# Expert stage of a hybrid transformer layer: sixteen expert steps become twelve, ranked on the chip, with six weight buffers

## What is computed

```python
scores = sigmoid(t @ router_w); biased = scores + router_b
grp = biased.reshape(n_tok, 4, 4)
g_sel = argmax(sum(top_k(grp, 2)))               # best group
idx = g_sel * 4 + top_k(grp[g_sel], 2)           # two experts of it
w = scores[idx] / sum(scores[idx])
y = sum_e gates[:, e] * ((silu(t @ w1[e]) * (t @ w3[e])) @ w2[e])
x = x + m5 * y
```

## Time and profile before

| | us |
|---|---|
| median of 3 runs | 928.34 |
| profiled execution, time | 927.07 |
| its span | 925.2 |
| PE busy | 865.7 |
| DVE busy | 383.7 |
| ACT busy | 197.6 |
| POOL busy | 122.8 |

### The profile page before, as it was taken

How to read it: one execution, slowest core, us unless ns; L and a number is a source line. 1 busy time by engine, 2 the same in 40 slices (tenths; PEclk the granted TensorE clock), 3 DMA queues, 4 the chain that set the end, 5 groups by cost and what they waited for, 6 DMA issues and landing times. The chain is left out here.

```text
span 925.2 us, 9791 instructions
## 1 busy us (share of the span) xinstructions
PE 865.7 (94%) x3803; PEld 459.7 (50%) x3803; DVE 383.7 (41%) x805; ACT 197.6 (21%) x435; POOL 122.8 (13%) x109
## 2 busy tenths in 40 slices
PE   4999999999999999999999999999993899999993
PEld 3445476655844445555555554444553444444441
DVE  3239455643345426556675750102236322222221
ACT  3221266100011032322332320100120222111110
POOL 1000000000148300110111111110001022221211
PEclk9899999999999999999999999999985899999997
DMA  8952020300072134262533435205142489999952
GB/s 313 330 193 91 0 91 1 115 1 1 1 250 76 39 99 153 91 205 60 184 98 134 147 136 198 91 0 182 45 168 83 155 269 300 299 305 289 308 148 41
DMA packets 79234, 131.65 MB, mean 142 GB/s; under 512 B 7297, under 2 KB 40786, under 8 KB 79186
## 3 DMA queue, kind: packets, MB, share of 16 engines
q1 hardware_dynamic: 74578, 122.61, 38.9%
q0 software_dynamic: 4608, 8.40, 4.0%
HBM read 126.79 MB, written 12.58 MB: 151 GB/s over the span
## 5 line engine op out<-in xcount | busy, mean ns | idle before, releaser
L468 PE MATMUL ps<-arena 128*128 128x512 f32 (+9 forms) x2962 | 770.6, 451 | 15.1 <-DVE arena L1593 5.7
L468 PEld LDWEIGHTS ps<-arena 128*128 128x128 f32 (+5 forms) x2962 | 360.3, 167 | 375.9 <-issue 355.2
L1022 ACT ACTIVATE arena<-ps 128x512 f32<-128x512 f32 (+5 forms) x132 | 54.7, 439 | 180.3 <-PE ps L468 133.3
L471 PE MATMUL ps<-tab,arena 128*128 128x128 f32 x476 | 67.4, 285 | 14.5 <-DVE arena L1266 6.6
L471 PEld LDWEIGHTS ps<-tab,arena 128*128 128x128 f32 x476 | 58.0, 148 | 42.7 <-issue 34.3
L1436 DVE SCALAR_TENSOR_TENSOR arena<-arena,ps 128x512 f32<-128x512 f32 x32 | 22.0, 687 | 116.7 <-ACT arena L1111 116.5
L1761 POOL TENSOR_TENSOR arena<-arena 128x512 f32<-128x512 f32 x24 | 30.4, 1268 | 279.8 <-DVE arena L1436 279.8
L1726 POOL TENSOR_TENSOR stat<-stat,mhalf 128x1 f32<-128x1 f32 (+2 forms) x20 | 23.2, 1162 | 319.0 <-DVE stat L1241 318.9
L1111 ACT ACTIVATE arena<-ps 128x512 f32<-128x512 f32 x32 | 19.1, 597 | 198.9 <-PE ps L468 198.9
L1684 DVE TENSOR_TENSOR arena<-arena,ps 128x256 f32<-128x256 f32 x16 | 6.7, 422 | 105.5 <-ACT arena L1213 105.5
L1404 DVE SCALAR_TENSOR_TENSOR arena<-arena,cond 128x512 f32<-128x512 f32 x56 | 42.6, 761 | 2.3 <-PE ps L471 0.6
(11 more groups left out here) (149 smaller groups left out, 379.0 us busy)
## 6 DMA issues: line engine op xcount, KB each, us to landing
arena<-in_moe_w SPq DMA_DIRECT2D x32, 1024.0 KB, 10.3
arena<-in_w_in SPq DMA_DIRECT2D x12, 2048.0 KB, 8.9
arena<-in_mod_w SPq DMA_DIRECT2D x16, 1024.0 KB, 5.2
arena<-in_moe_w SPq DMA_DIRECT2D x32, 512.0 KB, 10.7
arena<-in_mod_w SPq DMA_DIRECT2D x4, 2048.0 KB, 16.8
arena<-in_w_out SPq DMA_DIRECT2D x2, 2048.0 KB, 7.9
arena<-in_x SPq DMA_DIRECT2D x4, 512.0 KB, 5.7
arena<-in_w_in SPq DMA_DIRECT2D x2, 1024.0 KB, 18.3
```

The lines of the kernel that those rows point to most:

```text
L468: return nc.tensor.matmul(o, l, r, start=start, stop=stop, skip_group_check=True)
L471: return nc.tensor.transpose(o, i, ident[0:n, 0:n])
L1022: return A_(o, i, ACT.Copy)
```

## The change

The fourteen experts 2 to 15 are ranked on the chip by their number of tokens. Columns 0 and 1 are experts 0 and 1, columns 2 to 7 the six larger of the fourteen, columns 8 to 15 the eight smaller, in the order of their numbers. There are twelve steps: columns 0 to 7 have one each; columns 8 and 12, 9 and 13, 10 and 14, 11 and 15 share one. In a shared step slots 0 to 63 belong to the first expert and slots 64 to 127 to the second; the gather, the transposes, the modulation, silu, the scaling and the add handle both at once, and each matmul with expert weights becomes two, one for each half of the stationary columns, with its own weights and its own half of the PSUM partitions. If one of the eight smaller has more than 64 tokens, one more round follows, in which all sixteen run as before.

There are six weight buffers. Only experts 0 and 1 are loaded before the ranking is known. The other loads wait for `sort_ready`; SP reads each expert's number from `eid` into a register. Loads of columns 2 to 5 have no buffer to wait for, that of column n from 6 on waits for the outputs of the step that used buffer n - 6.

The token lists are made in groups of 2, 4, 4 and 2 steps. The group of experts 0 and 1 comes first; the ranking (`order_by_count`, `place_columns`) and the reordering of slots and gates by column (`permute`) follow on DVE between it and the first hidden layer; the picks of a later group are made one step ahead.

The first round is written out, where a loop stood before. The diff, cut to its core:

```diff
+HALF_CAP = P // 2
 NOBODY = 4096
+KNOWN = 2
+SINGLE = 8
+STEPS = SINGLE + (NE - SINGLE) // 2
+FREE = NE - KNOWN
+SLOTS = 6
+TOKEN_GROUPS = [(0, 2), (2, 4), (6, 4), (10, 2)]
...
+def step_parts(s):
+    if s < SINGLE:
+        return [(slice(0, P), s)]
+    return [(slice(0, HALF_CAP), s), (slice(HALF_CAP, P), s + (NE - SINGLE) // 2)]
+LOAD_COLUMNS = [c for s in range(STEPS) for _, c in step_parts(s)]
+def load_step(n):
+    return n if n < SINGLE else SINGLE + (n - SINGLE) // 2
+def token_group(s):
+    return max(f for f, (first, _) in enumerate(TOKEN_GROUPS) if first <= s)
...
-        at1 = [R_G] + [SLOT * ((N_OUT - 1 + i) % RING) for i in range(3)]
+        at1 = [R_G] + [SLOT * ((N_OUT - 1 + i) % RING) for i in range(3)] + [R_G + 3 * WE, R_QK]
         w13 = [region(a, 2, KD, FE) for a in at1]
         w2 = [[region(a, D), region(b, D)] for a, b in
-              ((R_G + 2 * WE, R_G + 2 * WE + D), (R1 + 2048, R1 + 3072), (2 * WE, SLOT + 2 * WE), (2 * SLOT + 2 * WE, R_V))]
+              ((R_G + 2 * WE, R_G + 2 * WE + D), (R1 + 2048, R1 + 3072), (2 * WE, SLOT + 2 * WE), (2 * SLOT + 2 * WE, R_V),
+               (R_G + 5 * WE, R1 + D), (R1, R1 + 4 * D))]
         rt = region(R_HC, 2048)
         masks = region(R_HC + 1280, P).bitcast(mybir.dt.bfloat16).rearrange("p (a n) -> p a n", a=2)
+        posP, gateP = rt[:, 320:384], rt[:, 980:1036]
+        eid = rt[:, 384:384 + FREE].bitcast(mybir.dt.int32)
...
-                if t == XT - 1:
-                    for n in range(N_OUT, N_LOADS):
-                        sp.wait_ge(ring_used[n % RING], used_value(n))
-                    load_expert(2, 2)
                 sp.wait_ge(xn2_done, t + 1)
                 sp.dma_start(xds[t], xn2[:, t]).then_inc(xs_done, 16)
                 sp.dma_start(os[t], xr[:, t]).then_inc(out_done, 16)
-            sp.wait_ge(hg_in[1], 16)
-            load_expert(3, 3)
-            def weights(r, first=0):
-                with sp.Fori(first, NE // 4) as i:
-                    for q in range(4):
-                        sp.wait_ge(y_mm, NE * r + 4 * i + (q - 3))
-                        load_expert(q, 4 * i + q)
-            weights(0, first=1)
-            sp.wait_ge(out_done, 16 * XT)
+            def expert_of(c):
+                return c if c < KNOWN else sp.value_load(eid[0:1, c - KNOWN:c - KNOWN + 1], min_val=KNOWN, max_val=NE - 1)
+            sp.wait_ge(sort_ready, 1)
+            for n in range(KNOWN, NE):
+                if n == KNOWN:
+                    for m in range(N_OUT, N_LOADS):
+                        sp.wait_ge(ring_used[m % RING], used_value(m))
+                if n == SLOTS - 1:
+                    sp.wait_ge(out_done, 16 * XT)
+                e = expert_of(LOAD_COLUMNS[n])
+                if n >= SLOTS:
+                    sp.wait_ge(y_mm, load_step(n - SLOTS) + 1)
+                load_expert(n % SLOTS, e)
...
+            def picks(f, e, parts):
+                for t in range(XT):
+                    for rows_of, c in parts:
+                        last = mm(ps[rows_of, (7 if f else 3), 5 * e:5 * e + 5], pick[:, e % PICKS, t, rows_of], tokg[:, t, c, :],
+                                  t == 0, t == XT - 1)
+                last.then_inc(pick_mm, 1)
...
+            def hidden(parts, slots):
+                for k in range(KD):
+                    for (rows_of, c), q in zip(parts, slots):
+                        last = mm(ps[rows_of, 2, :].rearrange("p (w f) -> p w f", w=2), hgT[:, k, rows_of], w13[q][:, :, k, :],
+                                  k == 0, k == KD - 1)
+                last.then_inc(h_mm, 1)
+            def outputs(par, parts, slots):
+                for half in range(2):
+                    for f in range(2):
+                        for (rows_of, c), q in zip(parts, slots):
+                            last = mm(ps[rows_of, 4 + 2 * par + half, :], aT[:, f, rows_of], w2[q][f][:, half * 512:(half + 1) * 512],
+                                      f == 0, f == 1)
+                last.then_inc(y_mm, 1)
...
+                pick_group(0)
+                turn_step(0)
+                for s in range(STEPS):
+                    for _, c in step_parts(s):
+                        n = LOAD_COLUMNS.index(c)
+                        pe.wait_ge(moe_in[n % SLOTS], 64 * (n // SLOTS + 1))
+                    pe.wait_ge(hgT_act, s + 1)
+                    pe.wait_ge(hgT_dve, s + 1)
+                    hidden(step_parts(s), slots_of(s))
+                    if s + 1 < len(TOKEN_GROUPS):
+                        pick_group(s + 1)
+                    if s + 1 < STEPS:
+                        turn_step(s + 1)
+                    if s >= 1:
+                        outputs_step(s - 1)
+                    pe.wait_ge(a_done, s + 1)
+                    turn_hidden()
+                outputs_step(STEPS - 1)
...
+            def split_gates(x, first, count):
+                hi, mid = tokg[:, :, first:first + count, 2], tokg[:, :, first:first + count, 3]
+                rest = rt[:, 400:400 + XT * count].rearrange("p (t e) -> p t e", t=XT)
+                link(V.tensor_copy(hi, x))
+                link(V.tensor_tensor(rest, x, hi, ALU.subtract))
+                link(V.tensor_copy(mid, rest))
+                V.tensor_tensor(tokg[:, :, first:first + count, 4], rest, mid, ALU.subtract).then_inc(tokb_ready, 1)
+            split_gates(gate[:, :, 0:KNOWN], 0, KNOWN)
...
+            def order_by_count():
+                link(V.scalar_tensor_tensor(key, total[:, KNOWN:NE], 64.0, erow, ALU.mult, ALU.add))
+                link(V.tensor_tensor(compare, key.unsqueeze(1).broadcast_to(wide), key.unsqueeze(2).broadcast_to(wide), ALU.is_gt))
+                link(V.tensor_reduce(order_of, compare, AX.X, ALU.add))
+            def place_columns():
+                bound = SINGLE - KNOWN - 0.5
+                link(V.scalar_tensor_tensor(key2, order_of, bound, erow, ALU.is_gt, ALU.add))
+                link(V.tensor_tensor(compare, key2.unsqueeze(1).broadcast_to(wide), key2.unsqueeze(2).broadcast_to(wide), ALU.is_le))
+                link(V.tensor_reduce(column, compare, AX.X, ALU.add))
+                link(V.tensor_tensor(chosen, const("iota")[:, 0:FREE].unsqueeze(2).broadcast_to(wide),
+                                     column.unsqueeze(1).broadcast_to(wide), ALU.is_equal))
+                link(V.tensor_tensor(compare, chosen, eidx.unsqueeze(1).broadcast_to(wide), ALU.mult))
+                link(V.tensor_reduce(eidf, compare, AX.X, ALU.add))
+                V.tensor_copy(eid, eidf).then_inc(sort_ready, 1)
+            def permute(o, x):
+                work = rt[:, 1040:1040 + XT * FREE * FREE].rearrange("p (t c e) -> p t c e", t=XT, c=FREE)
+                for t in range(XT):
+                    last = V.tensor_tensor(work[:, t], chosen, x[:, t:t + 1, KNOWN:NE].broadcast_to(wide), ALU.mult)
+                link(last)
+                link(V.tensor_reduce(o, work, AX.X, ALU.add))
...
+                link(V.tensor_scalar(small64[:, KNOWN:NE], order_of, SINGLE - KNOWN - 0.5, float(CAP - HALF_CAP), ALU.is_gt, ALU.mult))
+                link(V.tensor_tensor(small64, small64, total, ALU.add))
+                link(V.tensor_reduce(nmax[:, 0:1], small64, AX.X, ALU.max))
...
+            def first_experts():
+                make_first_picks(0, KNOWN)
+                order_by_count()
+                take_first_tokens(0)
+                place_columns()
+                permute(tE(posP)[:, :, KNOWN:NE], tE(posm))
+                link(V.tensor_copy(tE(posP)[:, :, 0:KNOWN], tE(posm)[:, :, 0:KNOWN]))
+                dve.wait_ge(hg_mm, 1)
+                modulate()
+                permute(gateP.rearrange("p (t e) -> p t e", t=XT), gate[:, :, :])
+                split_gates(gateP.rearrange("p (t e) -> p t e", t=XT), KNOWN, FREE)
+                make_first_picks(*TOKEN_GROUPS[1])
+                dve.wait_ge(xs_done, 16 * XT)
+                V.sem_inc(ys_done, 2)
+                def scale_step(s):
+                    dve.wait_ge(y_mm, s + 1)
+                    dve.wait_ge(gate_take, token_group(s) + 1)
+                    if s >= 2:
+                        dve.wait_ge(ys_out[s % 2], 16 * (s // 2))
+                    scale(s % 2, s)
+                for s in range(STEPS):
+                    dve.wait_ge(silu_ready, s + 1)
+                    hidden()
+                    if s + 1 < STEPS:
+                        dve.wait_ge(hg_mm, s + 2)
+                        modulate()
+                    if s + 1 < len(TOKEN_GROUPS):
+                        take_first_tokens(s + 1)
+                    if s >= 1:
+                        scale_step(s - 1)
+                    if s + 2 < len(TOKEN_GROUPS):
+                        make_first_picks(*TOKEN_GROUPS[s + 2])
+                    if s + 2 == len(TOKEN_GROUPS):
+                        count_rounds()
+                        link(V.tensor_scalar(tE(posP)[:, :, SINGLE:NE], tE(posP)[:, :, SINGLE:NE], float(CAP - HALF_CAP), None, ALU.add))
```

(80 more changed lines are left out.)

260 lines of the change are left out of this document (131 added, 129 removed).

## The result

The changed kernel takes 903.9 us (median of 3 runs, 902.5 to 904.0) against 928.34 us: a ratio of 0.973, 95% interval 0.969 to 0.977. The forecast was 916, with a range from 907. The profiled execution took 902.5 us with a span of 900.6 us, so as before 1.9 us lie around the span.

The account below looks back on a forecast made before the run. In the expert stage PE (11.40 us per expert) and the DMA queues (12.18 us) nearly coincide. Last weights at 880 + 14.9 + 2.5 + 15.4 = 912.8 us span, + 3.2 = 916.0 us; range 907 to 927.

Parts of the forecast that it names:

- The limit: Expert stage: PE could do an expert in 11.40 us, the DMA queues deliver one in 12.18 us; weight stream's start and length matter.
- Part 1, pairs on PE: Paired steps: two column halves run side by side, 11.40 us like a single step; PE's work falls by 45.6 us.
- Rival (a): Paired steps: column halves run one after the other, 21.7 us per step; time 927, no change; chance 0.05.
- The routing: Tokens per expert: the eight smallest of experts 2 to 15 hold at most 64, so the half-step limit is just kept.
- Rival (d): An extra round: a paired expert at 65 tokens makes all 16 experts run again; time near 1115; chance 0.04.
- (e): An unseen wait of the new order opens a stream gap of over 20 us; slower by some per cent; chance 0.04.
- Part 2 and the start of the stream: Ranking on VectorE: expert numbers ready at about 710.8; weight flow starts at 713, bounds 712 and 716.
- Part 3, the length of the stream: Weight stream of 14 experts with gathers and adds: 167 us from 713, last weights at 880, bounds 874 and 887.
- rival (c): Weight stream longer: starts at 716, last weights near 890, time 925 to 931, no change; chance 0.11.
- (b): Queues keep up and PE alone sets the pace: span 875, time 878; chance 0.03.
- How a gather costs: Gathers in the weight stream: 162.4 us in all if priced by number, 170.6 by rows; 167 taken, no row says which.
- Part 4, the tail: After the last weights: 14.9 + 15.4 us as before, plus 2.5 us for the last hidden group starting at low clock.

Follow-up runs that it names:

- late_stream: Changed kernel with SP holding the first ranked load until the tokens of step 1 are transposed; 917.1 us.
- tokens_first: Changed kernel with VectorE taking the last token group ahead of modulating the next tokens in step 2; 903.9 us, ratio 0.975.
- empty_gathers: Changed kernel with a second gather per step into a spare buffer, all 128 row numbers out of range; 904.2 us.
- double_gathers: Changed kernel with each of the twelve gathers issued a second time into a spare buffer, 1024 more rows; 919.0 us.
- four_known_early: Changed kernel with experts 0 to 3 loaded ahead, thirteen steps, and outputs of the last step but one ahead of the last hidden group; 894.0 us, ratio 0.965.

## Why the prediction came out as it did

- **The limit.** Right: the end is set by the weight stream, its start and its length (late_stream, tokens_first). I forecast a wait of about 10 us before each hidden group from step 8 on; there was none before step 8, and 2.50, 10.19 and 3.75 us before the other three.
- **Part 1, pairs on PE.** Right, 7.09 us against 7.03. Rival (a) is out, and so is the loss of some 3.7 us that the Trainium skill ("TensorE: Matmul & The Clock Gate", section on packing small matmuls) would have made likely.
- **The routing.** Right: twelve steps, no further round. Rival (d) did not happen, nor did (e).
- **Part 2 and the start of the stream.** Right within a microsecond: the expert numbers were ready at 710.6 (forecast 710.8), the first load went out at 711.58 (first bytes forecast at 713). Missed: gathers and token groups cost PE 5.8 us between steps 1 and 3 (28.6 us from one hidden group to the other, 22.9 before), 3.7 of them by the last token group (tokens_first). It lay under the stream, as I had said of the 0 to 2 us that I saw. The last two loads had their buffers 1.4 us ahead of their issue, not 10.
- **Part 3, the length of the stream: this step failed.** I put it at 167 us (bounds 162.4 and 170.6), and the last hidden group at 880. The queues' share fell off at 866 to 867, 154 us after 713; a thin rest ran on (111 and 61 GB/s in the next two microseconds), and the group started at 869.77, 156.8 us after 713. The mis-sized term is the price per expert. I read "one expert each 12.18 us" as what the queues can deliver. It was the pace of a loop through four buffers, in which the queues had a share of 0.94 with gaps, while the same queues show 1.00 and 1.02 in the earlier trace rows where weights flow alone. I even wrote "DMA share is 0.95, nothing spare" under rival (c), where 0.95 was the spare: at 1.02, 167 us become 156. That rival, and (b), are out. The bounds failed with the value, since both ends were made from the same 12.18 us; none came from the rate with the gaps taken out. Both parts of the price were too high. The first 30 us of the stream, mostly weights, ran at 345 GB/s (line 713 to 743 above), which is 9.12 us per expert instead of 9.45. The added gathers cost 16.6 us for 1024 rows, by which 1850 rows come to 30.0 us, where the sum by rows had 38.3. 14 x 9.12 + 30.0 = 157.7 us, an estimate that prices adds like gathers, which no run shows; measured were 156.8.
- **How a gather costs.** By rows rather than by number (empty_gathers, double_gathers). The split of the 12.18 us between weights and gathers, which I thought the open question, was the smaller error.
- **Part 4, the tail.** 30.8 us instead of 32.8: the last hidden group lost 1.5 us to the clock rather than 2.5 (48 matmuls in 11.95 us, against 24 full-width ones in 10.47), and the rest was 1 us shorter. The clock fell to 0.50 in the wait before step 10 (window 846 to 854), and step 10 took 8.69 us. What the Trainium skill says in "TensorE: Matmul & The Clock Gate" (HAM oscillation) holds here for the longer waits: steps 10 and 11 started slow after 10.19 and 3.75 us. I had all four paired steps start slow by it; step 8, without a wait, and step 9, after 2.50 us, did not (7.09 us each). The length of the wait alone doesn't sort them: in four_known_early the last hidden group was slow (8.78 us) after 2.56 us.

In the sum: 912.8 - 10.2 (last hidden group earlier) - 2.0 (tail) = 900.6 us, the span measured.

## What to carry to other kernels

"The engine waits for DMA" doesn't mean that the DMA queues are full: look at their share in the same stretch, and compare bytes per share with a stretch in which nothing holds them back. A pace read from a loop with few buffers is the pace of the loop; when a change adds buffers, work out the transfer time from the rate without gaps as well, and take it at least as a bound. And a change that halves an engine's steps doubles what each step takes from the buffers: here it was worth 2.7% with six of them and cost 3.2% with four.

## What the runs showed of the hardware

- Twelve gathers with 128 out-of-range rows each added 0.4 us to the stream of the full queues; the packets are counted all the same, the bytes are not (the software queue has 3456 packets in the changed kernel, 4608 before and 5184 in empty_gathers, at 8.40 MB in all three).
- The rate of the queues per unit of share was 315 to 327 GB/s in the five kernels whose windows stand above, while the averages of their stretches, 146 to 187 us long, went from 239 to 330 GB/s. In a short stretch of mostly weights it was higher (345 / 1.03 = 335, at 713 to 743 us).
- 1024 more gathered rows of 4 KB made the stream 16.6 us longer, about 1.3 times the time of their bytes at the 330 GB/s of the stream; up to 3.4 us of it may be the slightly lower share in that run.
- Two interleaved matmuls with 64 stationary columns each, in two halves of the array's columns, took the time of one full-width matmul: 32 in 7.09 us, against 16 in 7.03.
